# Attention scores of six head pairs from high and low parts on the whole TensorE array, values of two pairs in one step, and two ACT steps in another order

## What is computed

```python
q, k_c, v_c, k_s, v_s, k_w, v_w, g_nsa, conv_b, conv_c, conv_x, gate_a, gate_b = split(rms_norm(x) @ w_in)
# 8 heads of 64, 2 groups of keys and values; q, k_s and k_w are normed per head
o_cmp = softmax(q @ kc - slope * dist_c) @ vc     # keys and values compressed to 15 blocks
o_slc = softmax(q @ k_s - slope * dist) @ v_s     # 16 selected blocks of 64; with 256 tokens: all of them
o_win = softmax(q @ k_w - slope * dist) @ v_w     # window of 512; with 256 tokens: all earlier ones
o_nsa = g0 * o_cmp + g1 * o_slc + g2 * o_win
u = conv_c * conv_x; z = conv_b * conv(u)
x = x + (sigmoid(gate_a) * (o_nsa @ w_branch_a) + sigmoid(gate_b) * (z @ w_branch_b)) @ w_out
x = x + square(relu(rms_norm(x) @ w_up)) @ w_down
```

## Time and profile before

| | |
|---|---|
| median of 3 runs | 901.95 us (901.92 to 902.12) |
| the profiled execution | 901.26 us |
| its span | 899.2 us |
| PE busy | 892.7 us (99%), 4926 instructions |
| DVE busy | 706.0 us (79%) |
| ACT busy | 555.3 us (62%) |
| POOL busy | 43.2 us (5%) |
| granted TensorE clock | 0.999 of full speed over the span |
| chain of work that ended last | PE 99%, ACT 1% |
| attention of block 1, scores to values | about 70 to 179 us from the span's start |

### The profile page before, as it was taken

How to read it: one execution, slowest core, us unless ns; L and a number is a source line. 1 busy time by engine, 2 the same in 40 slices (tenths; PEclk the granted TensorE clock), 3 DMA queues, 4 the chain that set the end, 5 groups by cost and what they waited for, 6 DMA issues and landing times.

```text
span 899.2 us, 13582 instructions
## 1 busy us (share of the span) xinstructions
PE 892.7 (99%) x4926; PEld 767.0 (85%) x4926; DVE 706.0 (79%) x1381; ACT 555.3 (62%) x954; POOL 43.2 (5%) x54
## 2 busy tenths in 40 slices
PE   9999999999999999999999999999999999999997
PEld 7988877888888888888889998888889988888886
DVE  6888899789866666677998999999976786666665
ACT  7767878755644444456655657776745755754454
POOL 0410000000000000000010100100000000000000
PEclk9999999999999999999999999999999999999999
DMA  9977677676465555556798888487565377555551
GB/s 343 320 214 199 177 203 219 198 293 202 154 229 187 192 191 196 190 191 209 219 236 268 231 206 270 106 230 240 169 211 164 114 212 237 187 187 187 188 188 47
DMA packets 97218, 184.53 MB, mean 205 GB/s; under 512 B 8128, under 2 KB 18176, under 8 KB 96896
## 3 DMA queue, kind: packets, MB, share of 16 engines
q1 hardware_dynamic: 92128, 166.35, 56.1%
q0 software_dynamic: 4656, 16.78, 10.0%
q10 hardware_dynamic: 368, 0.52, 0.2%
HBM read 164.69 MB, written 1.05 MB: 184 GB/s over the span
## 4 chain that ended last, share of the span: by engine, by line
PE 99%; ACT 1%; issue 0%; DVE 0%; DVEq 0%; ACTq 0%
PE pb L523 97%; PE pb L527 1%; PE pb L738 1%; ACT SM L1400 0%; ACT wlo L1174 0%; ACT SM L1174 0%; ACT whi L1174 0%; ACT PTC L1174 0%; DVE XS L2617 0%; DVE XS L2625 0%; DVEq L59 0%; DVE DG L2359 0%; ACT MSQ L1757 0%; DVE ST L2603 0%; ACT CC L1174 0%
## 5 line engine op out<-in xcount | busy, mean ns | idle before, releaser
L1174 ACT ACTIVATE whi<-raw 128x1024 fp32r<-128x1024 f32 (+2 forms) x304 | 309.1, 1039 | 125.5 <-PE pb L523 112.5
L1787 DVE TENSOR_TENSOR wlo<-raw,whi 128x1024 fp32r<-128x1024 f32 (+1 forms) x267 | 315.7, 1211 | 78.7 <-ACT whi L1174 78.2
L523 PE MATMUL pb<-XT,whi 128*128 128x512 f32 (+1 forms) x1232 | 283.8, 358 | 0.0
L523 PE MATMUL pb<-whi,ZO 128*128 128x512 f32 (+1 forms) x776 | 238.9, 388 | 0.0
L523 PEld LDWEIGHTS pb<-XT,whi 128*128 128x128 f32 x1232 | 200.8, 189 | 23.8 <-issue 1.4
L523 PEld LDWEIGHTS pb<-whi,ZO 128*128 128x128 f32 x776 | 145.2, 188 | 29.7 <-issue 0.4
L523 PE MATMUL pb<-XT,wlo 128*128 128x256 f32 (+1 forms) x1032 | 166.4, 282 | 0.0
L523 PEld LDWEIGHTS pb<-XT,wlo 128*128 128x128 f32 (+1 forms) x1032 | 153.2, 190 | 14.0
L523 PE MATMUL pb<-whi,XT 128*128 128x512 f32 (+1 forms) x544 | 161.8, 389 | 0.0
L523 PE MATMUL pb<-wlo,ZO 128*128 128x512 f32 (+1 forms) x388 | 148.3, 387 | 0.0
L523 PEld LDWEIGHTS pb<-whi,XT 128*128 128x128 f32 x544 | 101.0, 188 | 20.7 <-issue 0.7
(11 more groups left out here) (258 smaller groups left out, 657.9 us busy)
## 6 DMA issues: line engine op xcount, KB each, us to landing
raw<-in_w_in SPq DMA_DIRECT2D x105, 512.0 KB, 4.8
raw<-in_w_ff SPq DMA_DIRECT2D x64, 512.0 KB, 5.3
raw<-in_w_up SPq DMA_DIRECT2D x32, 512.0 KB, 4.5
raw<-in_w_down SPq DMA_DIRECT2D x32, 512.0 KB, 4.8
wlo<-raw POOLq DMA_DIRECT2D x31, 512.0 KB, 5.8
raw<-in_w_branch_b SPq DMA_DIRECT2D x8, 512.0 KB, 5.3
raw<-in_w_out SPq DMA_DIRECT2D x8, 512.0 KB, 4.1
raw<-in_wx_kv SPq DMA_DIRECT2D x8, 512.0 KB, 5.4
```

Source lines behind the costliest of these rows:

```text
L523: return e.matmul(o, l, r, start=start, stop=stop, skip_group_check=True)
L1174: return e.activation(o, i, ACT.Copy, scale=scale)
L1787: e.tensor_tensor(wlo[u % NW][:, 0:c], raw_tile(u)[:, 0:c], whi[u % NW][:, 0:c].bitcast(F32), ALU.subtract).then_inc(lo, 1)
```

## The change

The change does five things, all in `attention1`.

1. Pairs 2 to 7 (`STACKED`: f = 1, 2, 3) get their scores from fp32r parts that lie in OT (shown as `ZO`). For each head the high part of its queries lies on its own 64 partitions and the low part on the other 64; the keys lie on both halves (group's head order swapped in the second copy), high parts in one set of columns, low parts in another. A matmul over all 128 partitions then sums high·key and low·key at once; one with the high keys and one with the low keys give the score. With b = 0 the first 128 queries are done for both kinds at once: 8 matmuls of 256 columns for the pair; with b = 1 only the second 128 queries remain: 4 matmuls. Before there were 4 fp32 matmuls for each pair, two of 128 and two of 256 columns.
2. The parts are made from TT: ACT copies the high parts (keys of group 0 at step 10, queries of f = 1 at 11, f = 2 at 13, keys of group 1 at 14, queries of f = 3 at 16), two instructions each, 64x512 for keys and 64x256 for queries; DVE subtracts for the low parts at steps 12, 14, 17, 20 and 24 in the same order (`k_low`, `q_low`). PE waits for them by `part_lo`.
3. Values go two pairs at a time: at 22 (0 and 1), 29 (2 and 3), 35 (4 and 5), 42 (6 and 7). There is a third PT buffer, and the block transposes of pair n wait for the values of two pairs earlier than before.
4. `turn_item(4)` writes to PB[7] instead of PB[6], and waits for ACT's copy PTC of the compressed branch, not for a `PT` copy.
5. `scale_p(0)` on ACT stands at step 13 directly behind the copy `PTC<-pb`, and no longer behind the next unit's `wlo` and `whi`.

Two semaphores that nothing waited for go. The diff, cut to its core:

```diff
-        PTP = [work(W0 + a, f"PT{i}", 768) for i, a in enumerate((12016, 14840))]
+        PTP = [work(W0 + a, f"PT{i}", 768) for i, a in enumerate((12016, 14840, 7216))]
...
+        STACKED = (1, 2, 3)
+        PARTS = ('k0', 'q1', 'q2', 'k1', 'q3')
+
+        def q_cols(f, p):
+            return slice(512 * f + 256 * p, 512 * f + 256 * p + 256)
+
+        def k_cols(g, l):
+            a = 2048 + 1024 * g + 512 * l
+            return slice(a, a + 512)
...
-        values_of = {a: (i,) for i, a in enumerate(pair_at[3:] + (35,))}
-        values_of[42] = (6, 7)
+        values_of = {22: (0, 1), 29: (2, 3), 35: (4, 5), 42: (6, 7)}
...
+        def turned_in(j):
+            return 7 if j == 4 else 6
...
                     def turn_item(j):
                         e.wait_ge(sc_p, j + 1)
-                        if j:
-                            e.wait_ge(pt_out, by_pe.index(j))
+                        if j == 4:
+                            e.wait_ge(pc_out, 1)
+                        elif j:
+                            e.wait_ge(pt_out, 4 if j == 5 else j)
...
                         if n:
                             e.wait_ge(sc_max, 2 * n)
-                        for p in range(2):
+                        if f in STACKED:
+                            e.wait_ge(part_lo, PARTS.index(f"q{f}") + 1)
+                            e.wait_ge(part_lo, PARTS.index(f"k{g}") + 1)
+                        for p in range(2) if f in STACKED else ():
+                            o, q = PB[4 + p], OT[:, q_cols(f, p)]
+                            for l in range(2) if b == 0 else ():
+                                kinds = OT[:, k_cols(g, l)].rearrange("p (b n) -> p b n", b=2)
+                                mm(o[:, 0:256].rearrange("p (b n) -> p b n", b=2), q[:, 0:128], kinds[:, :, 0:128],
+                                   l == 0, False)
+                            for l in range(2):
+                                i = mm(o[:, 256:512], q[:, 128:256], OT[:, k_cols(g, l)][:, 256 * b:256 * b + 256],
+                                       b == 1 and l == 0, l == 1)
+                            i.then_inc(sc_done, 1)
+                        for p in range(2) if f not in STACKED else ():
...
+                    for f in {11: (1,), 13: (2,), 16: (3,)}.get(s, ()):
+                        e.wait_ge(qk_out, 3)
+                        for p in range(2):
+                            r = slice(64 * p, 64 * p + 64)
+                            i = copy(OT[r, q_cols(f, p)], TT[r, TQ + f, :])
+                        i.then_inc(part_hi, 1)
+                    for g in {10: (0,), 14: (1,)}.get(s, ()):
...
+                            i = copy(OT[64 * p:64 * p + 64, k_cols(g, 0)],
+                                     TT[64 * p:64 * p + 64, i0:i0 + 2, :].rearrange("p i n -> p (i n)"))
+                        i.then_inc(part_hi, 1)
...
-                    if s - 4 in pair_of:
+                    if s == 13:
+                        scale_p(0, 0)
+                    if s - 4 in pair_of and s > 14:
                         scale_p(2 * pair_of[s - 4], 0)
...
-                if base + j >= 4:
+                if base:
                     e.wait_ge(pv_done, base + j - 3)
+                elif j >= 6:
+                    e.wait_ge(pv_done, j - 5)
...
+            def q_low(f):
+                e.wait_ge(part_hi, PARTS.index(f"q{f}") + 1)
+                for p in range(2):
+                    r, o = slice(64 * p, 64 * p + 64), slice(64 - 64 * p, 128 - 64 * p)
+                    i = e.tensor_tensor(OT[o, q_cols(f, p)], TT[r, TQ + f, :], OT[r, q_cols(f, p)].bitcast(F32),
+                                        ALU.subtract)
+                i.then_inc(part_lo, 1)
...
-                            e.wait_ge(pv_done, 2 * n - 2)
+                            e.wait_ge(pv_done, 2 * n - 4)
...
+                    for f in {14: (1,), 17: (2,), 24: (3,)}.get(s, ()):
+                        q_low(f)
+                    for g in {12: (0,), 20: (1,)}.get(s, ()):
+                        k_low(g)
```

## The result

The changed kernel takes 903.12 us (median of 22 runs, 901.85 to 904.05), the kernel before in the same comparison 901.91 (22 runs): a ratio of 1.0013, 95% interval 1.0007 to 1.0019. That is slower by 1.2 us, where 0.6 us faster was forecast, and 0.2 us above the range. It stays within 0.2%, as forecast, but the sign is the other one. So it neither went as forecast nor as one of the rivals alone.

The account below looks back on a forecast made before the run. PE's list was taken as the bound. Gross -2.27 us (steps -1.87, first wait -0.4), plus 1.05 at 88 us and 0.54 at step 19, gave -0.68: 901.3 us on the median, range 899.4 to 902.9.

Parts of the forecast that it names:

- The steps on PE: Matmul work on PE in steps 16 to 42, priced from the trace before: together -1.87 us.
- step 22: Pair with b = 0 on PE, values of pair 0 come in: from 2.51 to 3.25 us, +0.74.
- step 26: Pair with b = 1 on PE, values leave and two changes of shape go: -1.37 us.
- step 35: PE does values of two pairs instead of one: +0.65 us.
- the first wait: PE's wait for ACT's scaling at the first transposes, 81.92 us: goes as the scaling stands earlier, -0.4 us.
- that rival: Whole-array score matmuls each pay their weight load: 36 at 0.19, 6.8 us, 908.1 us, slower; chance 0.03.
- The wait of step 19: PE reaches the second transposes 1.28 us earlier and waits for ACT's scaling: +0.54 us.
- The wait at 88 us: PE waits for a bank of group x1, late through ACT's copies ahead of UU: 0.75 us, +1.05 with following banks.
- the pace: Three banks after the one at 88 us come at DVE's 0.80 against PE's 0.70: 0.10 us each.
- fit in the 2.87 us that ACT idles: ACT's copies of keys 0 and queries 1, 1.68 us, are hidden in its idle time ahead of 72.68 us.
- they cost nothing if that idle lies where they need it: DVE's low parts of keys 1 (1.2 us) and queries 3 (0.68) fall in a stretch with 3.1 us idle.
- DVE becomes the bound: Rival: from 88 us on no DVE idle is usable, PE's savings vanish into waits: 904.5 us, slower; chance 0.09.

Follow-up runs that it names:

- copies early: The change with ACT's high parts of keys 0, queries 1, queries 2 and keys 1 all made at steps 8 to 11; 902.45 us, ratio 1.0009.
- first wait alone: The kernel before with one edit, ACT's first scaling at step 13 directly behind the copy of the compressed branch; 901.30 us, ratio 0.9995.
- plain scores: The change with all scores by fp32 halves as before and no parts made; merged values and earlier first scaling stay; 900.93 us, ratio 0.9993.
- values apart: The change with values one pair a step and item 4 in PB[6], both as before; scores from parts stay; 903.58 us, ratio 1.0019.
- copies only: The change with parts made and waited for but not read, all scores by fp32 halves as before; 903.36 us, ratio 1.0017.
- no key lows: The kernel with copies early, without DVE's four subtractions for the keys' low parts; high parts used twice instead; 901.62 us, ratio 0.9996.
- four pairs: The change with scores from parts for pairs 4 to 7 only, ACT's copies at steps 9 to 11, subtractions at 17 and 20; 900.82 us, ratio 0.9984.
- low parts on POOL: The kernel with copies early, with all ten subtractions for low parts on POOL instead of DVE; 902.50 us, ratio 1.0005.
- lows twice: The change with two more 64x512 subtractions on DVE at step 20, 1.4 us of added work; 904.33 us, ratio 1.0032.

## Why the prediction was wrong

- **The steps on PE** were right in size: step 22 +0.74 (3.25 us against 2.51), step 26 -1.26 by PE's offsets up to the first matmul behind it (+1.62 to +0.36), where -1.27 was worked out ahead of 0.10 for the way out, step 35 +0.66 (1.89 against 1.23). So was the first wait. The weight loads stay hidden: eight `ZO` matmuls in 1.04 us. The rule of the Trainium skill ("TensorE: Matmul & The Clock Gate", Part 3) that loads overlap only where the row group differs, taken by itself, isn't borne out by this trace, and that rival fell.
- **The wait of step 19** was predicted as 0.54 us and is 0.42 in the trace, for the reason that was given.
- **The wait at 88 us** came where it was forecast, and only in part by the path that was forecast. The term was 0.75 us and 0.3 for the pace; PE starts that tile at 89.92, where the end of the one before would have let it start at 88.12: 1.80 us, and the four tiles from there take 0.2 more than before. Two steps failed. The 0.10 of overlap that was taken off each copy made ACT's copies of queries 2 and keys 1 1.68 us where they took 2.13; that 64 partitions take the full time, which was assumed, held. And DVE's low parts of keys 0 and queries 1 (1.42 and 0.88 us, not 1.20 and 0.68) were priced and never put on the path to that bank: that they "fit in the 2.87 us that ACT idles" looks at ACT alone. The kernel with copies early shows that DVE's work alone leaves 1.09 us, and without the keys' low parts 0.28. Another 0.26 us passes from the end of DVE's add to PE's start, which the term didn't have.
- **The wait at 177 us** was missing. The failed step is "they cost nothing if that idle lies where they need it", for the low parts of keys 1 and queries 3. The 3.1 us between DVE's busy time and 60 us were taken as room. DVE's timeline of before has only one wait in that stretch, of 0.47 us; the rest are short gaps between instructions:

```profile
122.54 1.23 DVE L1787 TENSOR_TENSOR wlo<-raw,whi 128x1024 fp32r<-128x1024 f32 x1 [0.47 <-ACT whi L1174]
```

Nor was the lateness at 88 us followed any further than PE's bank. DVE starts on the scores of pair 3 at 105.56 us before and at 107.74 after, 1.6 us later without the start, and on those of pair 7 2.2 us later. So most of this is carried over from 88 us; the low parts of keys 1 and queries 3 add 0.6 and fill the waits of DVE (1.04 us at 108 us, 0.47 at 122) that could have made up for it.

What this lateness does is read along the queues; the times in these rows are as they stand, with the start in them. DVE's first operation on the scores of pair 7 starts at 150.61 us before and at 153.41 after; ACT's exponentials wait for it, before as after, and pass the lateness on; ACT's low part of the awaited unit and POOL's DMA behind it come later. DVE before, and DVE after, then ACT before and ACT after:

```profile
150.61 0.29 DVE L1953 CUSTOM_DVE_ANT_0 SM<-pb,CST 128x128 f32<-128x128 f32 x1
```

```profile
153.41 0.29 DVE L2004 CUSTOM_DVE_ANT_0 SM<-pb,CST 128x128 f32<-128x128 f32 x1
```

```profile
151.29 0.40 ACT L1400 ACTIVATE SM<-SM,ST 128x128 f32<-128x128 f32 x1 [2.27 <-DVE ST L1953]
```

```profile
154.09 0.40 ACT L1448 ACTIVATE SM<-SM,ST 128x128 f32<-128x128 f32 x1 [2.26 <-DVE ST L2004]
...
166.72 1.04 ACT L1206 ACTIVATE wlo<-raw 128x1024 fp32r<-128x1024 f32 x1
```

POOL's issue of that DMA, in the view of the tile `wlo` from 164 us on, before (first fence; ns, first and last start, then us to landing) and after:

```profile
L2664 POOL DMA_DIRECT2D wlo<-raw x1: 862/862/862, 166.6 to 166.6; - x1
...
DMA to landing us min/median/max: 8.1/8.1/8.1
```

```profile
L2735 POOL DMA_DIRECT2D wlo<-raw x1: 862/862/862, 168.1 to 168.1; - x1
...
DMA to landing us min/median/max: 9.5/9.5/9.5
```

The landing moves from 174.7 to 177.6 us, by 1.4 us of issue (0.6 of them the start) and 1.4 of a longer transfer. PE wanted the part at 175.29 before and would have wanted it at 176.28 after. With the transfer of before it would have landed at 176.2 and PE wouldn't have waited: the lateness on DVE's list took up the slack, and the longer transfer made the wait. How long the transfer takes goes with its place among three loads of the next weights. Before (first fence), they go out from 164.68 to 166.2 us and the DMA behind all three; in the change it goes out between the second and the third:

```profile
164.68 1.52 SPq L449 DMA_DIRECT2D raw<-in_w_branch_a  x3
```

```profile
167.17 0.88 SPq L466 DMA_DIRECT2D raw<-in_w_branch_a  x2
168.42 0.37 SPq L466 DMA_DIRECT2D raw<-in_w_branch_a  x1
```

Eleven of the kernels here have that DMA. Behind the three loads it takes 8.1 us (the kernel before) and 8.4 (first wait alone); between the first and the third 9.1 to 9.6 (the change, copies early, plain scores, values apart, copies only, no key lows, four pairs); ahead of all three 7.7 (low parts on POOL, lows twice), and in these two PE doesn't wait at 177 us, though DVE starts on the scores of pair 7 1.6 and 3.5 us later than before (each less its start). With plain scores it is issued at 165.0, takes 9.5 us and lands just as PE comes. That fits the 0.71 us that were left without the keys' low parts. No run moved the DMA or the loads by themselves, so this is read from the traces and not shown by an edit.

- **The rivals.** "DVE becomes the bound" came true in part: PE's savings vanish into waits behind DVE's list, the second one by way of ACT, POOL and a DMA whose transfer became longer too. Its time, 904.5, was too high, since part of the work did fit: with queries 2, DVE's wait at 96 us fell from 1.63 us to 0.50. It was given 0.09.

In sum, -0.68 was forecast. In the two profiled executions PE is 1.8 us later behind these steps, without the start: the bank at 88 us takes 2.0 us with its pace instead of 1.05, the wait at 177 us 1.4 instead of nothing (1.16 of it in the list of waits), and step 29 0.1 more than its price. That accounts for the difference of 2.5 us. The medians of 22 runs give +1.2, and the interval of their ratio 0.6 to 1.7. Each trace is one execution, and the one of before lies 0.7 us under its median; which piece of the 1.8 is smaller in the other executions isn't known.

## What to carry to other kernels

A gain on the bounding engine is paid out only as far as the engines behind it keep up, so price each added instruction on every list up to the next place where that list really waits. Read room from the waits in an engine's timeline, not from the difference between a window and its busy time: 3.1 us of the one was 0.5 us of the other here. And follow a lateness past the first wait that it causes: the lists behind it carry it on. Parts for six pairs cost 2.4 us where the change puts them; parts for four, made in front of waits that DVE had anyway, cost nothing that shows once the last low part doesn't come by DMA.

## What was not expected of the hardware

- Neighbouring copies of 64 partitions on ACT and subtractions on DVE don't overlap as the 128-partition rows did: on ACT 0.64 us from start to start for 64x512 where 0.53 was taken, 0.42 for 64x256 where 0.31 was; on DVE 0.71 and 0.44 where 0.60 and 0.34 were. The two neighbours lie on different partitions; whether that is why wasn't tried.
- Work on POOL that reads SBUF stretched DVE operations of 0.17 us to 1.01 us, and a low part of 1.22 us to 2.32.
- PE went on 0.26 us after the end of the DVE add that freed its bank (89.14 + 0.42 to 89.83 in the kernel with copies early: 0.27), where the forecast counted nothing.
- The same DMA of one low part took 7.7 us ahead of three loads of weights, 8.1 and 8.4 behind them, and 9.1 to 9.6 among them.
